# A V table read once for four token tiles, as one dense product, in a hybrid encoder block

## The reference

```python
scores = jnp.einsum('thpd,hpnd->thpn', q, keys)
top_s, top_i = lax.top_k(scores, PEER_TOPK)
...                                     # 8 heads x 16 experts chosen per token
gate = jax.nn.softmax(best_s, axis=-1)
u = jnp.take(u_tab, e_blk, axis=0)
act = jax.nn.gelu(jnp.einsum('td,tkd->tk', h_blk, u), approximate=False) * g_blk
vv = jnp.take(v_tab, e_blk, axis=0)
y = jnp.einsum('tk,tkd->td', act, vv)
...
h = _layernorm(DEEPNORM_ALPHA * h + y, ln2_g, ln2_b)
```

## Time and profile before

| | |
|---|---|
| median of three runs | 3569.27 us |
| span of the profiled execution | 3575.8 us |
| PE busy | 2446.3 us (68%) |
| DVE busy | 2097.0 us (59%) |
| ACT busy | 655.0 us (18%) |
| POOL busy | 2209.1 us (62%) |
| moved by DMA | 1290.18 MB, mean 361 GB/s |
| of it by the POOL queue (gathers) | 1073.87 MB |

### The profile page before, as it was taken

How to read it: one execution, slowest core, us unless ns; L and a number is a source line. 1 busy time by engine, 2 the same in 40 slices (tenths; PEclk the granted TensorE clock), 3 DMA queues, 4 the chain that set the end, 5 groups by cost and what they waited for, 6 DMA issues and landing times.

```text
span 3575.8 us, 37418 instructions
## 1 busy us (share of the span) xinstructions
PE 2446.3 (68%) x12224; PEld 1513.4 (42%) x12224; DVE 2097.0 (59%) x4939; ACT 655.0 (18%) x1652; POOL 2209.1 (62%) x2093
## 2 busy tenths in 40 slices
PE   8889993677976876667977877766797730133354
PEld 6676872444754544434735544433564310000000
DVE  5134899875477675554358776554447669744400
ACT  3331322332022213321003212321101000000000
POOL 1000577677547765677556766677767667777774
PEclk9899996888998987777988988867898865566588
DMA  5323999899989999999999999999999999999998
GB/s 171 91 87 136 363 401 360 336 392 402 409 312 373 400 412 360 350 381 384 415 402 351 408 405 394 369 377 371 398 413 410 409 410 409 410 409 409 409 410 324
DMA packets 367626, 1290.18 MB, mean 361 GB/s; under 512 B 39596, under 2 KB 68148, under 8 KB 362308
## 3 DMA queue, kind: packets, MB, share of 16 engines
q0 software_dynamic: 294912, 1073.87, 76.8%
q1 hardware_dynamic: 66760, 201.33, 15.2%
q10 hardware_dynamic: 5760, 12.59, 0.9%
HBM read 1274.65 MB, written 12.98 MB: 360 GB/s over the span
## 4 chain that ended last, share of the span: by engine, by line
PE 24%; DMA 22%; POOL 17%; DVE 16%; issue 15%; ACT 3%; DVEq 3%; ACTq 0%; POOLq 0%; SPq 0%
DMA ring<-in_ev,idxT 12%; PE banks L1570 10%; POOL ring L818 8%; DVE ring L1260 8%; POOL ring L804 8%; DMA ring<-in_eu,eidx 5%; PE banks L1580 4%; PE banks L1559 4%; DMA arena<-in_eu,eidx 3%; PE banks L1855 2%; PE banks L1702 1%; PE banks L1621 1%; DMA wslot<-in_w_mix 1%; POOL arena L818 1%; POOL arena L804 1%
## 5 line engine op out<-in xcount | busy, mean ns | idle before, releaser
L804 POOL DMA_INDIRECT ring<-in_eu,eidx x938 | 1044.4, 1113 | 875.5 <-DVE eidx L1529 393.4
L818 POOL DMA_INDIRECT ring<-in_ev,idxT x894 | 950.9, 1064 | 380.0 <-issue 245.7
L1559 PE MATMUL banks<-ring,wide 128*32 128x512 f32 x3576 | 631.5, 790 | 530.5 <-DMA ring<-in_ev,idxT 460.5
L1260 DVE CUSTOM_DVE_ANT_0 ring<-ring,h_cur 128x1024 f32<-128x1024 f32 x663 | 782.6, 1221 | 192.1 <-DMA ring<-in_eu,eidx 190.1
L1570 PE MATMUL banks<-arena,wslot 128*128 128x256 f32 (+2 forms) x3280 | 747.2, 386 | 21.9 <-DMA wslot<-in_w_pq 12.5
L1570 PEld LDWEIGHTS banks<-arena,wslot 128*128 128x128 f32 (+1 forms) x3280 | 622.4, 194 | 179.2 <-issue 70.9
L1559 PEld LDWEIGHTS banks<-ring,wide 128*32 128x32 f32 x3576 | 120.1, 130 | 851.7 <-DMA ring<-in_ev,idxT 431.5
L1260 DVE CUSTOM_DVE_ANT_0 ring<-ring,banks 128x1024 f32<-128x1024 f32 x275 | 329.3, 1217 | 110.8 <-DMA ring<-in_eu,eidx 106.8
L1580 PE MATMUL banks<-arena 128*128 128x128 f32 x1408 | 216.2, 312 | 42.3 <-ACT arena L995 26.1
L1580 PEld LDWEIGHTS banks<-arena 128*128 128x128 f32 x1408 | 202.9, 223 | 79.7 <-ACT arena L995 33.5
L1559 PE MATMUL banks<-arena,wide 128*32 128x512 f32 x520 | 138.6, 868 | 118.6 <-DMA ring<-in_ev,idxT 64.5
(11 more groups left out here) (302 smaller groups left out, 2810.9 us busy)
## 6 DMA issues: line engine op xcount, KB each, us to landing
wslot<-in_w_pq SPq DMA_DIRECT2D x64, 576.0 KB, 8.3
wslot<-in_w_mix SPq DMA_DIRECT2D x24, 1536.0 KB, 9.8
wslot<-in_w_qkv SPq DMA_DIRECT2D x48, 512.0 KB, 7.0
wslot<-in_w_fqk SPq DMA_DIRECT2D x32, 512.0 KB, 7.6
ring<-in_eu,eidx POOLq DMA_INDIRECT x938, 12.6
wslot<-in_w_out SPq DMA_DIRECT2D x7, 2048.0 KB, 10.4
ring<-in_ev,idxT POOLq DMA_INDIRECT x894, 12.4
wslot<-in_w_z SPq DMA_DIRECT2D x16, 512.0 KB, 6.7
```

Source lines behind the costliest of these rows:

```text
L804: pool.indirect_dma_start(out=place(UPOS[k]), out_offset=None, in_=eu, in_offset=bass.IndirectOffsetOnAxis(ap=eidx[:, n % (2 * TT), c // T ...
L818: pool.indirect_dma_start(out=place(VPOS[k]), out_offset=None, in_=ev, in_offset=bass.IndirectOffsetOnAxis(ap=idxT[:, n % (2 * TT), t:t + ...
L1260: dve.tensor_tensor_reduce(out=row, in0=row, in1=hp[0] if held else h_cur[:, n % 3, :] if n < NT - TT else hp[n % 2], scale=1.0, scalar=0. ...
L1559: last = pe.matmul(BY[k][32 * j:32 * j + 32, :], wide32[:, at:at + 32], place(VPOS[4 * q + j])[:, k * 512:(k + 1) * 512], start=(m == 0), ...
```

## The change

Tiles 2 to 5 (`DENSE`, blocks 1 and 2) no longer gather V rows. For each of their 512 tokens a 128x128 matrix is made that holds the token's 128 weights at the place of the expert's number (row: number / 128, column: number mod 128). It is the product of two one-hot matrices on PE: DVE compares an iota with the row numbers and multiplies with the weight (L1407, one instruction per token), ACT squares iota minus the column number and takes the positive part of 1 minus that (L951 per token, L953 per four tokens). Four tokens make one PE step (L1709); ACT copies the result out, regrouped, to a staging buffer (L941), and stores 16 tokens at a time to DRAM (`d_act`, 1.05 MB per store).

When all 512 are stored and the units are over, SP reads the V table once, in 128 blocks of 128 experts (0.524 MB each, eight slots in `wslot`), and the activations in 16 chunks of 2.1 MB, in pieces of 512 B. PE multiplies each block with the activations of all four tiles: eight products of 128x128 by 128x512 per block, into all eight PSUM banks (L1722), adding up over the 128 blocks. The sums come out transposed; ACT copies them to SBUF and PE transposes them back. Tiles 0, 1, 6 and 7 (`ONE_BY_ONE`) gather V rows as before; tiles 6 and 7 do it after the dense product, since that holds the banks.

The ring has 13 places in the units instead of 18, since staging and one-hot buffers take five; later there are 20 instead of 27. `pace()` now spreads the first 768 dots up to the last `idx` instead of up to the last block's choosing. By its table tile 2's spreading opens at step 381, step 583 has 772 dots and 384 of the 512 tokens spread, the rest are spread in steps 584 to 599, and the dense product opens at step 604 with 856 dots done.

```diff
-NR = 18
-NX = 9
-NU, NQ = 16, 8
+PLACES = 18
+NR = 13
+NX = 7
+DENSE = range(2, 6)
+ONE_BY_ONE = [n for n in range(NT) if n not in DENSE]
+HOT = range(P * DENSE[0], P * (DENSE[-1] + 1))
+STAGED = 16
+CHUNK = 8
+NCHUNK = P // CHUNK
+NV = 8
+NU, NQ = 12, 5
...
+        if HOT[0] <= toks[-1] <= HOT[-1]:
+            ready, step = edge - P + (dots[s] - edge) * P // (P - 24), 8
...
+            if dense[-1] < P or dense[max(0, s - 6)] < P:
+                ready = toks[-1]
+        dense.append(min(P, dense[-1] + 2) if built and s > built + 3 else 0)
...
 # SP, after its units
+            sp.wait_ge(s_ixT, transposed(NT - 1))
+            for i in range(P):
+                c = i // CHUNK
+                if i % CHUNK == 0:
+                    if c == 0:
+                        for k in range(2):
+                            sp.wait_ge(s_stored[k], 16 * (len(HOT) // STAGED // 2))
+                    if c >= 2:
+                        sp.wait_ge(s_spot, len(HOT) // 4 + CHUNK * (c - 1))
+                    sp.dma_start(chunk[c % 2], d_act[:, :, c * CHUNK * STAGED:(c + 1) * CHUNK * STAGED].rearrange("g j x -> j g x")
+                                 ).then_inc(s_chunk[c % 2], 16)
+                if i >= NV:
+                    sp.wait_ge(s_spot, len(HOT) // 4 + i - NV + 1)
+                sp.dma_start(vtab[i % NV], ev[i * P:(i + 1) * P, :]).then_inc(s_w[i % NV // 4][i % 4], 16)
...
 # POOL, at the first gather into the wide places
                 if p == WIDE:
-                    pool.wait_ge(s_hTe, TT * NB)
-                    pool.wait_ge(s_h1st, 16 * NB)
+                    for k in range(2):
+                        pool.wait_ge(s_stored[k], 16 * (len(HOT) // STAGED // 2))
+                    pool.wait_ge(s_spot, len(HOT) // 4)
+                    pool.wait_ge(s_ixT, transposed(NT - 1))
...
 # ACT, in experts(s)
+                for k in range(hot(TOKS[max(0, s - 3)]) // STAGED, hot(TOKS[max(0, s - 2)]) // STAGED):
+                    act.wait_ge(s_sev, STAGED // 4 * (k + 1))
+                    act.dma_start(d_act[k, :, 0:P * STAGED], staged[k % 2]).then_inc(s_stored[k % 2], 16)
+                for q in range(hot(TOKS[max(0, s - 2)]) // 4, hot(TOKS[s - 1]) // 4):
...
+                    act.activation(staged[k % 2].rearrange("p (i t) -> p t i", t=STAGED)[:, 4 * m:4 * m + 4, :],
+                                   BY[q % 2][:, :].rearrange("p (t i) -> p t i", t=4), ACT.Copy).then_inc(s_sev, 1)
+                for q in range(hot(TOKS[s - 1]) // 4, hot(TOKS[s]) // 4):
...
+                    for r in range(4):
+                        act.activation(ones_at[q % 2][:, r, 0, :], iota[:, :], ACT.Square, bias=cols[:, 4 * m + r:4 * m + r + 1])
+                    act.drain()
+                    act.activation(ones_at[q % 2][:, :, 0, :], ones_at[q % 2][:, :, 0, :], ACT.Relu, scale=-1.0, bias=1.0).then_inc(s_w32, 1)
...
 # DVE, in experts(s), behind the dots of the step
+                for q in range(hot(TOKS[s - 1]) // 4, hot(TOKS[s]) // 4):
+                    spots(q)
...
+                for r in range(4):
+                    t = 4 * m + r
+                    last = dve.tensor_scalar(ones_at[q % 2][:, r, 1, :], iota[:, :], rows_[:, t:t + 1], dots[:, n % 2, t:t + 1],
+                                             ALU.is_equal, ALU.mult)
+                last.then_inc(s_hot, 1)
...
 # PE, in experts(s)
-                for q in range(TOKS[s - 1] // 4, TOKS[s] // 4):
+                for q in range(hot(TOKS[s - 1]) // 4, hot(TOKS[s]) // 4):
+                    pe.wait_ge(s_hot, spotted(q))
+                    pe.wait_ge(s_w32, columns(DENSE[q // 32]) + 1 + q % 32 + 1)
+                    if q >= 2:
+                        pe.wait_ge(s_sev, q - 1)
+                    for r in range(4):
+                        last = pe.matmul(BY[q % 2][:, r * P:(r + 1) * P], ones_at[q % 2][:, r, 0, :], ones_at[q % 2][:, r, 1, :],
+                                         start=True, stop=True)
+                    last.then_inc(s_spot, 1)
+                for i in range(DONE[s - 1], DONE[s]):
...
+                    acts = chunk[c % 2][:, :, STAGED * ii:STAGED * (ii + 1)]
+                    for k in range(KB):
+                        last = pe.matmul(B[k][:, :], vtab[i % NV][:, k * P:(k + 1) * P], acts, start=(i == 0), stop=(i == P - 1))
+                    last.then_inc(s_spot, 1)
```

More of the change, by code:

```diff
@@ L125, in pace @@
     last = UNITS.index(("idx", NB - 1, 0))
-    alone = UNITS.index(("top", NB - 1, 0))
-    total = sum(share(kind, b) for kind, b, i in UNITS[first + 1:alone])
+    total = sum(share(kind, b) for kind, b, i in UNITS[first + 1:last])
     second = UNITS.index(("att", 1, 0))
     levels = sum(share(kind, b) for kind, b, i in UNITS[first + 1:second])
-    dots, toks = [0], [0]
+    dots, toks, dense = [0], [0], [0]
     ready, run, lately = 0, 0.0, 0
@@ L142, in pace @@
         else:
-            run += share(kind, b) if n < alone else 0.0
+            run += share(kind, b) if n < last else 0.0
             if n < second:
@@ L172, in pace @@
     summed = [next(s for s in range(len(toks)) if toks[s] >= P * (n + 1)) for n in range(NT)]
-    for n in range(NT):
+    for n in ONE_BY_ONE:
         for f in range(2, 32 // PHASE):
             assert phase_step(toks, n, f) < next(s for s in range(len(toks)) if toks[s] > P * n + 4 * PHASE * f)
+    for n in range(NT):
+        assert begun[n] > dotted[n] and (n == 0 or begun[n] > summed[n - 1])
+    for n in DENSE:
+        assert summed[n] < next(s for s in range(len(dots)) if dots[s] > P * (n + 2))
+        summed[n] = dense.index(P) + 1 + n - DENSE[0]
+    assert begun[DENSE[-1] + 1] - 1 > summed[DENSE[0]]
+    assert toks[UNITS.index(("sel", NB - 1, 0))] >= P * NT - 2 * T
     fetch = []
@@ L196, in pace @@
                 place += 1
-    return dots, toks, dotted, begun, summed, fetch, upos, vpos
-DOTS, TOKS, DOTTED, BEGUN, SUMMED, FETCH, UPOS, VPOS = pace()
+    return dots, toks, dense, dotted, gelu, begun, summed, fetch, upos, vpos
+DOTS, TOKS, DONE, DOTTED, GELU, BEGUN, SUMMED, FETCH, UPOS, VPOS = pace()
+DENSE_AT = next(s for s in range(len(DONE)) if DONE[s])
 U_AT, V_AT = {p: k for k, p in enumerate(UPOS)}, {p: k for k, p in enumerate(VPOS)}
 def slots():
-    begin = UNITS.index(("top", NB - 1, 0)) + 1
     at = UPOS + VPOS
-    wide = min([UPOS[k] for k in range(DOTS[begin], P * NT)] + [VPOS[k] for k in range(TOKS[begin], P * NT)])
+    wide = min([UPOS[k] for k in range(DOTS[DENSE_AT], P * NT)] + [VPOS[k] for k in range(alone(TOKS[DENSE_AT]), len(VPOS))])
     turns, slot, before, held = list(range(NR)), [], [], {}
```

203 lines of the change are left out of this document (151 added, 52 removed).

## The result

The changed kernel takes 4521.23 us (median, 4518.07 to 4525.59) against 3571.68 us before: 1.265 times as long, 95% interval 1.2625 to 1.2672. The forecast was 4190 us, so the direction was right and the loss was 331 us too small; the range ended at 4420. The profiled execution has a span of 4516.3 us.

A forecast was written before the change was run, and what follows sets the result against it. The prediction took the kernel to be bound by 2048 gathers on DMA. Its terms, 1530 + 1290 + 110 + 30 + 906 + 20 + 301 + 10, summed to 4197 us, forecast as 4190, range 3950 to 4420.

The forecast's parts named there:

- B: Units from tile 2's opening to the last index: 1290 us, bounds 898 to 1500.
- E: The dense product, 128 blocks of eight products on PE with loads hidden beside it: 906 us.
- A: From the start up to tile 2's opening, bound by DMA: 1530 us, bounds 1480 to 1630.
- C: Spreading the other 128 tokens in 16 steps after the units: 110 us, bounds 100 to 160.
- F: After the dense product, copies, 32 transposes, one evacuation and tile 6's weights; with G and H's label only, 20 us.
- G: V gathers of tiles 6 and 7, 236 remaining at the earlier pace: 301 us, bounds 285 to 345.
- H: From the last V product to the end of the kernel: 10 us.
- rival 2: Dense product starves if a chunk lands later than 56.6 us; at 70 us, E 1120 us, total 4400; 12%.
- the cheap price of the V strips: Dense product paid like V's strips, 0.24 us a product: E 246 us, total 3530, faster than before; 3%.
- Rival 3: Steps in turn cost more, units longer at 1.2 GHz: B 1400 to 1550 us, total 4300 to 4450; 9%.
- D: Last store, then load of the first chunk, before the dense product: 30 us, bounds 10 to 60.
- rival 1: Units fall to DVE's floor, dots running ahead: B 900 to 1130 us, total 3800 to 4030; 15%.

The follow-up runs named there:

- the half product: From the changed kernel, 126 of the 128 dense blocks multiply only four of their eight column parts, all loads kept; 4206.86 us.
- the 16-bit one: One-hot products a step later, one-hot rows ahead of the dots, plus bfloat16 one-hot matrices, activations and V rows, against the changed kernel; 3726.35 us.
- the run with both orders: One-hot columns made on VectorE, against the kernel with one-hot products a step later and one-hot rows ahead of the dots (4148.75 us); 4168.31 us.

## Why the prediction was wrong, step by step

**What bounds it afterwards: right.** With 512 gathers gone, DMA is at 0.58 and 0.57 in B and E, and the gathers saved came back as a product that little overlaps. E was forecast 906 us from the earlier trace rows and is 921 us; the half product shows that it lies on the path once the gathers are over, and the 16-bit one that it falls to the traffic when its price falls.

**A, C, E, F, G, H: right**, within 18 us each. The rival of the starved dense product came only in small: beside the gathers six chunks took 44 to 69 us, four of them more than the 56.6 us of its condition, and PE stood 29 us of E for V loads; once the gathers are over a chunk lands in 10.5 us, still twice the 5.1 us worked out in rival 2. What did not come is the cheap price of the V strips: the 32-bit product cost 0.87 us (0.43 a record), not 0.24. One reading of the prediction is off without consequence: behind 2902 us the kernel before issues 240 U gathers, not 256.

**B: the step that failed.** I wrote that if all spreading were in turn B would be 1330 us, "elsewhere steps gain, because the wait for V rows goes", and took 1290. It is 1540. In the sum PE is busy 733 us with the units and 98 with the one-hot products, 831 together, and stands 459 of the 1290. Measured, it is busy 992 us (179 of them one-hot products) and stands 548. So 161 of the missing 250 us are matmuls that took longer than they were priced, and 89 are standing. With the products a step later the units take 731 us of PE again, as reckoned, and the one-hot products 139: it is the turn that made the matmuls dear, and the sum had priced them as if PE did not stand. Three things were left out, and all were in reach.

First, 1330 was no ceiling. For the other steps it took DVE's busy time alone, which has no wait in it, so "elsewhere steps gain" had nothing to take off. In the earlier trace rows the longest engine was busy 1064 of 1391 us, and only 237 us of the other 327 were waits for V rows. The units themselves are partly in turn.

Second, the durations came from a stretch at a granted clock of 0.85. Where PE stands 7 us in a step, the four products take 2.08 us at a granted clock of 0.50 (1.2 GHz), against 1.05 with the products a step later at 1.00 (2.4 GHz); over B the granted clock was 0.75 against 0.82, and PE was busy 122 us longer with the same records.

Third, ACT's part was let hide beside DVE's, with the copy-out at 0.59 us where it took 1.04. Taking the squares and the positive part out shortened B by 56 us, although 76 us of work were added on DVE.

Rival 3 named this with the clock as its sign, gave it 1400 to 1550 us for B, and 9% of the chance. The mechanism was rightly seen, as the merge step shows (17.4 us forecast, 19 to 20 measured); its size over all units was not. The total lies over rival 3's range because C, D, E and G were longer too, by some 75 us together.

**D: too small.** 63 us for 30, and over its bound of 60. The 2 MB load that it was taken from did run beside gathers, but in packets of 16 KB; the chunk comes in 512 B, and between C and E, where the U gathers run at full rate, it took 51.0 us. The 64 KB row has such pieces; D took it as a time, while rival 2 took it as a price per piece.

**The floor of DVE (rival 1) did not come,** in the changed kernel or with the product a step later: there B is 1185 us, with DVE busy 878 of them, and 74 us more of DVE in the run with both orders did not move it.

## What to carry to other kernels

When work is added to a chain of steps, look where each engine has to wait within the step: a product that needs the same step's rows puts two engines in turn, and moving it one step later gave back 361 us here without removing an instruction. Sum such a stretch from what it takes now, with its present waiting, and not from the busy time of its engines; and take the price of a matmul at the clock that the new gaps will leave it. A transfer issued into a stretch where others fill the DMA engines is priced from a row with the same company and the same size of packet: the same 2 MB took 10 to 12 us in 16 KB packets and 44 to 69 us in 512 B ones.

## What the hardware showed that was not expected

A 128x512 copy from PSUM that writes its elements scattered took 2.38 us in 16 bit and 1.04 us in 32 bit, and 0.59 us when four 16-bit elements go together and the bank is read at a stride of 512 bytes instead, the same as the plain 32-bit copy of that shape. The order of the walk was worth a factor of four.

A load of 2 MB in pieces of 512 bytes took 10.5 us to land in quiet and 44 to 69 us beside gathers, with some 395 GB/s moved in all. The same bytes in packets of 16 KB took 10.4 to 11.8 us beside gathers, with some 415 GB/s moved in all.
